# A branch product in seven block products instead of eight, with the sums of its inputs made beforehand

## What is computed

```
y = stack over 4 groups of (causal mean of xp over a window - xp)   # 1024 x 512
y = einsum('bsgc,gcd->bsgd', y, w_group) * pool_scale               # 1024 x 512
y_pool = y @ w_branch_pool                                          # 512 x 1024 weights
m = sigmoid(g_pool) * y_pool + sigmoid(g_sb) * y_sb                 # y_sb: attention branch
```

## Time and profile before

| | |
|---|---|
| median of 3 runs | 1949.68 us (1949.53 to 1949.8) |
| profiled execution | 1950.04 us |
| its span, first to last instruction | 1948.3 us |
| TensorE busy | 1926.2 us, 99% |
| VectorE busy | 1303.9 us, 67% |
| ScalarE busy | 768.2 us, 39% |
| mean granted clock of TensorE | 0.999 |

### The profile page before, as it was taken

One profiled execution on the slowest core, in us unless ns is written; L12 is line 12 of the kernel. 1 busy time (PEld: TensorE's weight loads), 2 busy tenths in 40 slices (PEclk: granted clock), 3 DMA queues, 4 the chain that ended last, 5 costly groups with the idle time before them and its releaser, 6 DMA issues.

```text
span 1948.3 us, 25383 instructions
## 1 busy us (share of the span) xinstructions
PE 1926.2 (99%) x9248; PEld 1617.4 (83%) x9248; DVE 1303.9 (67%) x1608; ACT 768.2 (39%) x1152; POOL 135.9 (7%) x218
## 2 busy tenths in 40 slices
PE   7999999999999999999999999999999999999998
PEld 7888888888888799888888888888888888888887
DVE  5978767774566644125777777888777776755555
ACT  6423232333434423224666552365232332324344
POOL 1000000000000100001333330010000000000002
PEclk9999999999999999999999999999999999999999
DMA  4456654568675532346645447643444553667655
GB/s 148 154 195 226 225 174 152 182 206 312 204 238 194 169 109 65 108 138 197 171 137 161 125 140 257 194 152 109 146 167 157 176 182 130 223 247 254 204 194 205
DMA packets 244148, 347.21 MB, mean 178 GB/s; under 512 B 15968, under 2 KB 149856, under 8 KB 239200
## 3 DMA queue, kind: packets, MB, share of 16 engines
q1 hardware_dynamic: 244064, 346.09, 54.2%
HBM read 232.79 MB, written 112.98 MB: 177 GB/s over the span
## 4 chain that ended last, share of the span: by engine, by line
PE 95%; DVE 2%; issue 1%; DMA 1%; ACT 1%; POOL 0%; SPq 0%; POOLq 0%; DVEq 0%; ACTq 0%
PE bank L1019 38%; PE bank L1116 15%; PE bank L1063 8%; PE bank L1064 8%; PE bank L1065 8%; PE bank L981 5%; PE bank L1182 4%; PE bank L1158 2%; PE bank L1252 2%; PE bank L965 1%; PE bank L1269 1%; PE bank L1268 1%; PE bank L1239 1%; PE bank L1237 1%; DVE tail_p L2235 0%
## 5 line engine op out<-in xcount | busy, mean ns | idle before, releaser
L1765 DVE TENSOR_TENSOR dn_lo<-dn_lo_raw,dn_hi 128x1024 fp32r<-128x1024 f32 x149 | 181.8, 1224 | 149.9 <-ACT dn_hi L1448 149.3
L1019 PE MATMUL bank<-hi_t,wa_hi 128*128 128x512 f32 x640 | 249.0, 389 | 0.2 <-issue 0.2
L1019 PE MATMUL bank<-lo_t,wa_hi 128*128 128x512 f32 x640 | 249.0, 389 | 0.0
L1019 PE MATMUL bank<-hi_t,wa_lo 128*128 128x512 f32 x640 | 249.0, 389 | 0.0
L1448 ACT ACTIVATE dn_hi<-dn_lo_raw 128x1024 fp32r<-128x1024 f32 x149 | 158.0, 1061 | 217.0 <-DMA dn_lo_raw<-act_dram 216.7
L1063 PE MATMUL bank<-dn_hi 128*128 128x512 f32 x596 | 232.8, 391 | 1.0 <-DVE dn_lo L1765 1.0
L1064 PE MATMUL bank<-dn_hi,dn_lo 128*128 128x512 f32 x596 | 231.9, 389 | 0.0
L1065 PE MATMUL bank<-dn_lo,dn_hi 128*128 128x512 f32 x596 | 231.9, 389 | 0.0
L1019 PE MATMUL bank<-hi_b,wa_hi 128*128 128x512 f32 x480 | 186.8, 389 | 0.5 <-DVE up L1889 0.5
L1019 PE MATMUL bank<-lo_b,wa_hi 128*128 128x512 f32 x480 | 186.7, 389 | 0.0
L1019 PE MATMUL bank<-hi_b,wa_lo 128*128 128x512 f32 x480 | 186.7, 389 | 0.0
(11 more groups left out here) (201 smaller groups left out, 3590.5 us busy)
## 6 DMA issues: line engine op xcount, KB each, us to landing
wa_lo_raw<-in_ffn_w_gate_up_dram SPq DMA_DIRECT2D x88, 512.0 KB, 4.9
dn_lo_raw<-act_dram SPq DMA_DIRECT2D x149, 256.0 KB, 4.3
act_dram<-g SPq DMA_DIRECT2D x44, 512.0 KB, 4.7
wd_t<-in_ffn_w_down_dram SPq DMA_DIRECT2D x44, 512.0 KB, 6.6
act_dram<-s_of SPq DMA_DIRECT2D x88, 256.0 KB, 6.6
wd_dram<-wd_t SPq DMA_DIRECT2D x22, 1024.0 KB, 6.0
dn_lo_raw<-wd_dram SPq DMA_DIRECT2D x85, 256.0 KB, 3.2
dn_lo_raw<-in_ffn_w_down_dram SPq DMA_DIRECT2D x64, 256.0 KB, 2.9
```

The lines of the kernel that those rows point to most:

```text
L1019: last = nc.tensor.matmul(acc, lhs, rhs, start=n == 0 and i != 2 and i < 5, stop=n == 11, skip_group_check=True)
L1765: return nc.vector.tensor_tensor(dst, raw, hi.bitcast(f32), ALU.subtract)
```

## The change

The pool branch product is made in four units of two output tiles each, in place of two units of four tiles. The first unit (`pool_branch_plain`) makes its four banks plainly, in banks 4 to 7. The other three (`pool_branch_unit`) use PRODUCTS: seven products of half the depth, 3 x 2 = 6 matmuls each, alternating between banks 0 to 3 and 4 to 7. VectorE makes four sums of the weight blocks for each of these units (`pool_weight_sums`) and, once, four sums of the branch inputs (`first_sum_of_y`, `sums_of_y`) in yt_raw, which ScalarE and VectorE split into yt_hi and yt_lo (`sums_of_y_hi`, `sums_of_y_lo`). ScalarE writes the raw inputs of the second pair of groups into yt_raw in `take_group(1)`. A unit's four results are put together from the banks by ScalarE (`first_pool_part`, `second_pool_part`) and VectorE (`pool_c11`, `pool_c22`, `pool_c12`, `pool_c21`) in pst and pool_part. The weight loads are 2 x 256 KB per unit (before 2 x 512 KB), and the order of loads and stores on SyncE is a new one. pst moves to another address.

In the diff `...` stands where lines are left out: semaphore declarations, and bodies of helpers that repeat a pattern shown. `sums_of_y_hi(slot, sums)` waits for yt_sum >= sums and copies one slot of yt_raw (1024 columns) to yt_hi. `split_pool_plain` copies, or subtracts, the two halves of 512 columns of the plain unit. `first_sum_of_y` makes two sums and one difference of 1024 columns, `sums_of_y` three differences. `pool_c12(u)` and `pool_c21(u)` add bank place 2 or 3 to pool_part, into pst[2] or pst[1], after the sixth or the seventh product.

```diff
--- before.py
+++ after.py
@@ -71,7 +71,7 @@
 U_P, U_V = [[n + 2 * m for m in range(2)] for n in range(2)]
 U_B = U_V[1] + 1
-U_QK = U_B + 2
+U_QK = U_B + KT // 2
 U_GATE = U_QK + 4
 U_C = U_GATE + KT
@@ -81,7 +81,7 @@
     if g < U_B:
         return [Q_P[0], Q_V[0], Q_P[1], Q_V[1]][g]
     if g < U_QK:
-        return Q_B + 2 * (g - U_B) + 1
+        return Q_B + g - U_B
     return Q_QK + g - U_QK
@@ -339,7 +339,10 @@
         y_lo = at("y_lo", [P, 2, SEQ], f32r, o + 8192)
         wg_raw = at("wg_raw", [P, 4, P], f32, o + 16384)
-        pst = at("pst", [P, 4, HALF], f32, o)
+        pst = at("pst", [P, 4, HALF], f32, base + 144 * K)
+        yt_lo, yt_raw = both("yt_lo", [P, 4, BR // 2, HALF], base + 112 * K)
+        yt_hi = at("yt_hi", [P, 4, BR // 2, HALF], f32r, base + 128 * K)
+        pool_part = at("pool_part", [P, HALF], f32, G0)
         assert o + 18432 <= W0 and X0 + 32768 + 57344 <= W0 and G0 + DM * FB <= nc.sbuf_usable_end
         bank = ctx.enter_context(nc.psum_tensor("bank", [P, 8, HALF], f32))
@@ -443,6 +446,14 @@
         sum_ok = sem("sum_ok")
         yhi = sem("yhi")
         ylo = sem("ylo")
...
         gate_ready = sem("gate_ready")
         gate_free = [sem(f"gate_free{b}") for b in range(2)]
         z_ok = sem("z_ok")
@@ -524,6 +535,11 @@
         def gate_place(n, th):
             return gates_odd[:, th] if n % 2 else w_raw[:, th].rearrange("p a k f -> p (a k f)")[:, BR * P:BR * P + 2 * HALF]
+        def pool_block(w, par, slot, n=1):
+            return w[:, par, slot // 4, 2 * (slot % 4):2 * (slot % 4 + n), :]
         @block.sync
@@ -753,9 +769,7 @@
                 sp_.wait_ge(whi, g - 1)
                 sp_.wait_ge(wlo, g - 1)
                 for ab in range(2):
-                    t = 4 * u + 2 * ab
-                    sp_.dma_start(w_raw[:, g % 2, ab].rearrange("p (k t) f -> p k t f", t=2),
-                                  bp_cols[:, :, t:t + 2, :]).then_inc(raw_in[g % 2], 16)
+                    sp_.dma_start(pool_block(w_raw, g % 2, 6 * ab, 2), bp_cols[:, :, 2 * u + ab, :]).then_inc(raw_in[g % 2], 16)
             def spill_v():
                 for b in range(4):
@@ -769,21 +783,26 @@
                 for part, t_ in ((0, qk_hi), (1, qk_lo)):
                     sp_.dma_start(qk_dram[part, m], t_[m % 2][:, :].bitcast(f32)).then_inc(qk_sp[m], 16)
-            def spill_pool_branch(m):
-                for b in range(4):
-                    sp_.wait_ge(acc_free[b], Q_B + m + 1)
-                    sp_.dma_start(g_dram[2 * m + b % 2, b // 2, :, 2, :], pst[:, b, :]).then_inc(y_sp[b], 16)
+            def spill_pool_branch(u):
+                for b in (0, 3, 2, 1) if u else range(4):
+                    if u == 0:
+                        sp_.wait_ge(acc_free[b], Q_B + 1)
+                    elif b == 3:
+                        sp_.wait_ge(pool_mid, 2 * u)
+                    else:
+                        sp_.wait_ge(acc_free[(1, 3, 2)[b]], Q_B + u + 1)
+                    sp_.dma_start(g_dram[2 * u + b % 2, b // 2, :, 2, :], pst[:, b, :]).then_inc(y_sp[b], 16)
             spill_v()
-            pool_branch_unit(0)
-            pool_branch_unit(1)
+            for u in range(KT // 2):
+                pool_branch_unit(u)
+            spill_pool_branch(0)
             mix_cols(U_QK, QC, KC)
+            spill_pool_branch(1)
             mix_cols(U_QK + 1, QC + 1, KC + 1)
-            spill_pool_branch(0)
-            spill_pool_branch(1)
-            mix_cols(U_QK + 2, QC + 2, KC + 2)
             spill_pool_branch(2)
             spill_pool_branch(3)
+            mix_cols(U_QK + 2, QC + 2, KC + 2)
             mix_cols(U_QK + 3, QC + 3, KC + 3)
             spill_qk(0)
             spill_qk(1)
@@ -1183,24 +1202,53 @@
                                             (rhs_lo if p == 1 else rhs_hi)(kt), start=n == 0, stop=n == 3 * BR - 1)
                 last.then_inc(acc_ready, 1)
-            def pool_branch_quad(m):
-                u = m // 2
+            def pool_branch_plain():
+                pe.wait_ge(whi, U_B + 1)
+                pe.wait_ge(wlo, U_B + 1)
+                for b in range(4):
+                    cols = slice(b // 2 * HALF, (b // 2 + 1) * HALF)
+                    branch_sum(4 + b, lambda w, kt: pool_block(w, U_B % 2, 6 * (b % 2) + kt // 2)[:, kt % 2, :],
+                               lambda kt: yp_hi[:, kt, cols], lambda kt: yp_lo[:, kt, cols], groups_of=b // 2 * 2)
+            def pool_branch_unit(u):
+                par, s = (U_B + u) % 2, (u + 1) % 2
                 pe.wait_ge(whi, U_B + u + 1)
                 pe.wait_ge(wlo, U_B + u + 1)
-                for b in range(4):
-                    wait_bank(b, Q_B + m)
-                    cols = slice(b // 2 * HALF, (b // 2 + 1) * HALF)
-                    branch_sum(b, lambda w, kt: w[:, (U_B + u) % 2, m % 2, 2 * kt + b % 2, :],
-                               lambda kt: yp_hi[:, kt, cols], lambda kt: yp_lo[:, kt, cols],
-                               groups_of=b // 2 * 2 if m == 0 else None)
+                for i in range(7):
+                    place, _, slot, (kind, block_) = PRODUCTS[i]
+                    if i in (0, 1, 3, 4):
+                        wait_bank(place, Q_B + u - 1)
+                    if i == 2:
+                        pe.wait_ge(pool_copied, u)
+                        pe.wait_ge(yt_lo_ok, 2)
+                    if u == 1 and i == 4:
+                        pe.wait_ge(yt_lo_ok, 3)
+                    if u == 1 and i == 6:
+                        pe.wait_ge(yt_lo_ok, 4)
+                    if i >= 5:
+                        pe.wait_ge(pool_mid, 2 * (u - 1) + i - 4)
+                    for n in range(3 * BR // 2):
+                        kt, p = n // 3, n % 3
+                        if kind == "b":
+                            rhs = (yp_lo if p == 1 else yp_hi)[:, 2 * (block_ > 0) + kt, block_ // 2 * HALF:(block_ // 2 + 1) * HALF]
+                        else:
+                            rhs = (yt_lo if p == 1 else yt_hi)[:, block_, kt, :]
+                        last = nc.tensor.matmul(bank[:, 4 * s + place, :], pool_block(w_lo if p == 2 else w_hi, par, slot)[:, kt, :], rhs,
+                                                start=n == 0 and i != 2 and i < 5, stop=n == 3 * BR // 2 - 1, skip_group_check=True)
+                    if i < 6:
+                        last.then_inc(pool_prod, 1)
+                    else:
+                        last.then_inc(acc_ready, 4)
             for m in range(2):
                 unit_quad(U_P[m], U_P[m] % 2, Q_P[m], fresh=m == 0)
                 v_quad(m)
                 group_quad(m)
-            for m in range(KT // 2):
-                pool_branch_quad(m)
+            pool_branch_plain()
+            for u in range(1, KT // 2):
+                pool_branch_unit(u)
             for m in range(4):
                 unit_quad(U_QK + m, (U_QK + m) % 2, Q_QK + m)
@@ -1613,15 +1661,51 @@
                 for b in range(4):
                     g, th = 2 * m + b % 2, b // 2
                     act.wait_ge(acc_ready, 4 * Q_G[m] + b + 1)
-                    nc.scalar.activation(yp_hi[:, g, th * HALF:(th + 1) * HALF], bank[:, b, :], ACT.Copy,
-                                         scale=pscale[:, g:g + 1]).then_inc(ev_hi, 1)
-            def stage_pool_branch(m):
-                for b in range(4):
-                    act.wait_ge(acc_ready, 4 * (Q_B + m) + b + 1)
+                    last = nc.scalar.activation(yp_hi[:, g, th * HALF:(th + 1) * HALF], bank[:, b, :], ACT.Copy,
+                                                scale=pscale[:, g:g + 1])
                     if m:
-                        act.wait_ge(y_sp[b], 16 * m)
-                    nc.scalar.activation(pst[:, b, :], bank[:, b, :], ACT.Copy).then_inc(acc_free[b], 1)
+                        if b == 0:
+                            act.wait_ge(ylo, 4)
+                        last = nc.scalar.activation(yt_raw[:, 1 + th, g - 2, :], bank[:, b, :], ACT.Copy, scale=pscale[:, g:g + 1])
+                    last.then_inc(ev_hi, 1)
+            def stage_plain(b):
+                act.wait_ge(acc_ready, 4 * Q_B + b + 1)
+                nc.scalar.activation(pst[:, b, :], bank[:, 4 + b, :], ACT.Copy).then_inc(acc_free[b], 1)
...
+            def split_pool_unit(u):
+                act.wait_ge(pool_sum, 4 * u)
+                split_static(U_B + u)
+            def first_pool_part(u):
+                act.wait_ge(pool_prod, 6 * (u - 1) + 1)
+                act.wait_ge(y_sp[0], 16 * u)
+                nc.scalar.activation(pst[:, 0, :], bank[:, 4 * ((u + 1) % 2), :], ACT.Copy).then_inc(pool_copied, 1)
+            def second_pool_part(u):
+                act.wait_ge(pool_prod, 6 * (u - 1) + 3)
+                if u > 1:
+                    act.wait_ge(acc_free[3], Q_B + u)
+                nc.scalar.activation(pool_part[:, :], bank[:, 4 * ((u + 1) % 2), :], ACT.Copy).then_inc(acc_free[0], 1)
             take_pool(0)
             split_static(U_P[1])
```

(52 more changed lines are left out.)

70 lines of the change are left out of this document (added).

## The result

The kernel after takes 1953.66 us (median of 19 runs, 1952.04 to 1956.59), the kernel before 1949.53 beside it: ratio 1.0021, 95% interval 1.0015 to 1.0028, or +4.1 us. Forecast were +0.96 and 1950.6 within 1946.9 to 1953.4: the sign was right, the size was not, and the time lies 0.3 us above the range.

The account below looks back on a forecast made before the run. TensorE was taken to bound the kernel: -4.08 us for 18 fewer matmuls, +1.36 for unit 1 and +3.68 for units 2 and 3 gave +0.96, so 1949.68 became 1950.6 us, range 1946.9 to 1953.4.

Parts of the forecast that it names:

- TensorE bounds the branch, 18 matmuls are worth 4.08 us: Pool branch product: 174 matmuls instead of 192 at 0.2267 us each, the whole gain, -4.08 us.
- VectorE ahead of the group product is hidden: Before the branch: take_v comes 4.05 us later, but bank 0 is free 2.3 us before TensorE wants it.
- (e): Rival: VectorE late ahead of the group product by more than 2.3 us, +1 to +3 us; chance 0.02.
- Unit 1: First block unit: its store lands after 3.75 us, delaying the copy and the sixth product to 783.56; +1.36 us.
- The ring: Units 2 and 3: split, store landing, copy and next splits repeat every 11.36 us against TensorE's 9.52; +3.68 us, chance 0.60.
- That store takes 5.5 us to land: Store of pst[0] behind a 1 MB load pair on SyncE, priced at 5.5 us against 2.0 with nothing ahead.
- rival (c): The store gating each unit lands later still; landings of 6.1 us pass +3.9, 8 us gives +7.7, 1957; chance 0.08.
- The clock: Branch stalls: granted clock expected to stay 1.00, as in two stretches with stalls of 0.7 and 1.05 us.
- (d): Rival: TensorE's clock falls to 1.2 GHz in the branch's short stalls; +19 us in units 2 and 3, 1970; chance 0.02.
- The sum for the branch: Pool branch, first matmul at 764.62 to its end at 809.10, against 808.14 before: +0.96 us.
- From there on all moves together: Everything behind the branch and its moved loads was to shift unchanged, with no further gain or loss.
- rival (a): The gating store is not late, landing 2.0 us after issue; 9.76 us a unit, -2.64 us, 1947.0; chance 0.25.

Follow-up runs that it names:

- e5: Kernel after with stores ahead of weight loads, split ahead of copy in units 2 and 3, and unit 6's weight sums made early; 1947.32 us, ratio 0.9988.
- a_again: Kernel after, unchanged, measured again; 1953.48 us, ratio 1.0020 to the kernel before.
- e6: Kernel after with only the next unit's split put ahead of the bank place 0 copy and pool_c11 in units 2 and 3; 1951.03 us, ratio 1.0010.
- q2: Kernel before with 224 more do-nothing instructions (satisfied waits) on TensorE in its branch; 1950.78 us, ratio 1.0003.
- b_again: Kernel before, unchanged, measured again as a control; 1949.73 us, ratio 1.0000.
- p1: Kernel before with 63 more do-nothing instructions on VectorE at the end of its pool branch; 1949.38 us, ratio 1.0000.
- p4: Kernel before with 16 more do-nothing instructions on TensorE at the end of the branch; 1949.64 us, ratio 1.0001.
- q3: Kernel after with 31 more do-nothing instructions on TensorE in units 2 and 3; 1953.11 us, ratio 1.0018 to the kernel before.
- e2: Kernel after with a second place for pst[0], used by units 1 and 3, SyncE's order kept; 1948.94 us, ratio 0.9997 to the kernel before.
- Experiment 6: Runs adding do-nothing instructions on TensorE or VectorE to the kernel before, the kernel after and the version with all three cures; 1945.97 to 1953.11 us.
- e3: Kernel after with an unused 512 KB transfer added ahead of the stores of units 1 and 2; 1957.19 us, ratio 1.0041 to the kernel before.

## Why the prediction was wrong

*TensorE bounds the branch, 18 matmuls are worth 4.08 us.* Right. With all but the shortest waits gone (e5) the branch falls from 43.5 to 40.0; the plain unit took the forecast 10.88 us, the 126 matmuls of the block units 29.13 where 28.56 were reckoned.

*VectorE ahead of the group product is hidden.* Right: the branch started 764.90, 0.28 us later than before, with no wait for v; (e) did not happen.

*Unit 1.* Structure right, one term too small. ScalarE's timeline of the kernel after:

```profile
763.01 0.69 ACT L1664 ACTIVATE yp_hi<-bank,pscale 128x512 fp32r<-128x512 f32 x1
763.60 0.68 ACT L1669 ACTIVATE yt_lo_raw<-bank,pscale 128x512 f32<-128x512 f32 x1
764.17 0.69 ACT L1664 ACTIVATE yp_hi<-bank,pscale 128x512 fp32r<-128x512 f32 x1
```

The copies of take_group stand 0.57 to 0.59 us apart. I had priced them at 0.49, the spacing of another ScalarE copy in the earlier trace rows, one without a scale from a bank into pst; the row of the very copies there (2.77 us for four, with waits in it) gave no better price and should have been a bound. VectorE's last yp_lo started 767.78 instead of 766.8, the split of unit 5 ended 774.26 instead of 773.30, its store was issued 775.29 instead of 774.41. The landing, taken as 3.75 between 2.0 and 5.5, was 3.85. Everything of unit 1 is 1.05 us late: sixth product 784.61, forecast 783.56; of that 0.28 is the later start.

*The ring.* The first step that failed is "That store takes 5.5 us to land", used for both turns. The first took 6.48 (6.67 in a_again, 6.34 in e6), the second 5.56 (5.60). The periods were 12.41 and 11.50 us for 11.36: +1.05 and +0.14. That is rival (c) in kind, and mostly short of its point (6.1 us in both turns, with 5.5 in unit 1, where 3.85 was measured). The prediction's estimate from the Trainium skill, "DMA: Bandwidth & Descriptors" (Anatomy of one DMA), put the ring at 9.82 us; the measured 12.41 and 11.50 us speak against using that figure for a store behind other transfers.

What makes the first turn a microsecond longer is again a packet of instructions. In the kernel after one comes at 789.0 us, while the store of 785.08 is under way; none comes between 797.49 and 803.05. The control is q2, whose branch is that of the kernel before and where only TensorE's instruction count is another: its second store behind a q/k load, issued at 792.37, met a packet at 797.1. The DMA view of q2, 792.3 to 792.45 and 797 to 797.3:

```profile
g_dram<-pst SPq DMA_DIRECT2D x1, 256.0 KB, 6.9
...
q8 instruction: 1, 0.02, 21.8%
```

The same store in the kernel before, with no packet in its time, DMA view 792.4 to 792.6:

```profile
g_dram<-pst SPq DMA_DIRECT2D x1, 256.0 KB, 5.5
```

Ten profiles have the two stores right behind 1 MB of q/k loads and nothing else (before, b_again, p1, p4, q2, after, a_again, q3, e2, e6). The fourteen stores without a packet between issue and landing took 5.42 to 5.63 us, the six with one 6.34 to 6.85. 21.8% of 16 engines for 0.3 us is 1.05 us of one DMA engine, which is about the microsecond that is lost; that it is lost by waiting behind the packet on that engine is not shown. So the term was mis-sized in one of its two turns, by 0.98 us, because of something that no row shown to the prediction held: where TensorE's instruction packets fall.

*The clock.* "Against it: two stretches with stalls of 0.7 and 1.05 us have a granted clock of 1.00" rested on stretches whose stalls were shorter than those of the change. After a gap of 2.3 us between matmul starts (789.97 to 792.29) eight matmuls ran at 0.43 us apart, the 1.2 GHz level, and a_again has the same, with 0.67 in the stretch 792 to 796.5. The Trainium skill, "TensorE: Matmul & The Clock Gate" (A second HAM failure mode), tells of a clock that swings with micro-idles between groups of matmuls; the trace agrees for this one stretch, with 0.62 in it and 1.00 on both sides. It cost TensorE 8 x 0.2 = 1.6 us of its own time but not the branch: the next product that had to wait, unit 3's third, waited for the store until 803.1 anyway. q3, the kernel after with idle instructions, shows 1.00 throughout those stretches and the same branch, 46.3 us. And of the 19 executions of the kernel after two had a mean granted clock of 1.000 instead of 0.998 or 0.999; they took 1953.66 and 1954.11 us, no less than the median. So (d) came in part, at a price near nothing.

*The sum for the branch.* Forecast length 809.10 - 764.62 = 44.48, measured 46.51. Of the 2.03 us, 0.77 are unit 1 (1.05 less the start), 1.05 and 0.14 the ring, 0.08 the tail.

*"From there on all moves together."* This is the second step that failed, and it was argued from no row at all. The difference of the medians was missed by 3.2 us (4.13 against 0.96). In the profiles the branch is 2.0 us over its forecast and the last down projection 1.85 us longer, where nothing was forecast; the profiled executions lie 5.1 us apart, 0.9 more than the medians, so of the 3.2 us some 2 are the branch and the rest, about 1.1, falls to the projection. Experiment 6 shows what moves there. The cure of the ring therefore gave less than its forecast too: rival (a)'s 1947.0 became 1948.7 and 1948.9, with the branch at 41.6 for 40.9 (the weight sums of unit 6, which unit 1's lateness had pushed) and the projection at 210 to 211.

What stays open: why one load of the projection takes 0.3 to 0.9 us longer to land in the padded kernels with the change; how a packet of instructions makes a store or an issue slow; and why the clock fell in two runs of the kernel after and in none with longer stalls.

## What to carry to other kernels

When a change turns a relaxed buffer reuse into a wait, follow the whole way of the transfer that frees it, from the engine that its queue waits for to its landing, and cut it by the order of the queue or by a second place: here either was worth over 4.5 us of the branch, and the change without it was a loss. Price a landing from rows with the same traffic ahead, and let its range reach above the longest of them: an instruction packet in its time added a microsecond here. And when a kernel with fewer instructions gets slower far from the edit, follow the wait back to the transfer that it hangs on, and see whether a packet has moved onto it or onto the issues ahead of it, before looking for a dependence.

## What was new about the hardware

- A clock fall after one short idle: 2.3 and 2.5 us between matmul starts, in both profiles of the same kernel, at the same place. But e3 had gaps with waits of 3.29 and 2.46 us and kept a granted clock of 1.00; its stretch of the same window:

```profile
792.00:796.50 4.50, 4.25 (x18) 3.17 (x18) 3.54 (x3) 2.17 (x2) 0.00 (x0) 1.00 0.01 4
```

- A packet of instructions is one cause of a slow DMA issue, not the only one. In the last projection, up to the late loads, 43 of SyncE's issues in the 18 profiles took over 0.9 us (0.95 to 1.97, usually 0.33 or 0.43), and each had a 16 KB packet within 0.4 us of its start. But other packets met an issue that took its 0.43 us (the kernel before, 134.4 us into the projection), and in the whole kernel before 40 issues took over 0.9 us, 7 of them with a packet.
- The time of the packet follows TensorE's instruction count: 13 more bring it 1.5 us forward, 16 more 3, 31 more 3, 62 more 7 (each to half a us at either end), 224 more 3 us back, as 32 fewer would if one packet holds 256. That number is an estimate: 128 matmuls at 0.2267 us, with a weight load each, take 29.0 us, and the packets come 27 to 30 us apart. 63 on VectorE don't move it.
- A 256 KB store behind 1 MB of loads landed in 5.42 to 5.63 us fourteen times, and in 6.34 to 6.85 us the six times that a packet of instructions came between its issue and its landing. The packet took some 1.05 us of one of the 16 DMA engines.
